# One sequence's recurrent branch recorded behind its attention instead of beside the other's, in batches of two units, and the channel mixer's buffers laid out anew

## What is computed

```
u = rms_norm(h, norm_mix);  proj = u @ w_in        # 1792 wide: q 512 | k 128 | v 128 | xl 512 | gl 512
q, k = rope(rms_norm(q)), rope(rms_norm(k))        # 8 query heads, 2 kv heads, head_dim 64
attn = softmax(q k^T / 8) v                        # no mask, 2048 keys
xc = conv4(xl)                                     # depthwise, centred
for direction in (forward, backward):              # the recurrent branch (RG-LRU)
    r, i = sigmoid(xc @ w_r + b_r), sigmoid(xc @ w_i + b_i)      # block diagonal
    a = exp(-8 r softplus(-lam));  y = scan(a, sqrt(1 - a^2) * (i * xc))
lru = (y_fwd + y_bwd) * gelu(gl)
h = h + concat(rms_norm(attn), rms_norm(lru)) @ w_out
u = rms_norm(h, norm_ffn);  h = h + (silu(u @ w_gate) * (u @ w_up)) @ w_down     # 2816 wide
```

## Time and profile before

| | us |
|---|---|
| median of 3 runs | 2006.09 (2005.65 to 2009.26) |
| the profiled execution | 2005.26 |
| its span, slowest core (core 0) | 2003.7 |
| spans of the eight cores | 1988.4 to 2003.7 |
| TensorE busy | 1791.1 (89%) |
| ScalarE busy | 1074.5 (54%) |
| VectorE busy | 1013.3 (51%) |
| POOL busy | 359.2 (18%) |

### The profile page before, as it was taken

The page is one execution under the profiler, slowest core; times in us unless marked ns, Lnnn a source line. Parts: engine busy times, 40 slices in busy tenths (PEclk is TensorE's granted clock), DMA queues, the critical chain, the costliest instruction groups (busy, mean ns, idle before and its releaser), DMA issues.

```text
span 2003.7 us, 24506 instructions; the slowest of 8 cores (1988.4 to 2003.7 us)
## 1 busy us (share of the span) xinstructions
PE 1791.1 (89%) x8168; PEld 716.1 (36%) x8168; DVE 1013.3 (51%) x1249; ACT 1074.5 (54%) x1350; POOL 359.2 (18%) x396
## 2 busy tenths in 40 slices
PE   6996656866669999999899999999999999999997
PEld 2442212311113333333333334444444444444443
DVE  3477999947884142221522352383473653535331
ACT  4668787799988788766766773121121221113010
POOL 2123654455451221121000000000000000000000
PEclk9998777978789999999999999999999999999999
DMA  8754432572227677685533355476585675664633
GB/s 180 210 155 138 141 99 90 163 188 88 77 69 205 142 155 158 146 206 147 164 89 89 88 159 180 149 225 199 146 267 168 197 230 149 204 196 145 200 108 100
DMA packets 149127, 310.98 MB, mean 155 GB/s; under 512 B 19696, under 2 KB 28016, under 8 KB 149008
## 3 DMA queue, kind: packets, MB, share of 16 engines
q1 hardware_dynamic: 119696, 228.56, 39.1%
q0 software_dynamic: 29312, 80.86, 15.7%
HBM read 263.05 MB, written 69.99 MB: 166 GB/s over the span
## 4 chain that ended last, share of the span: by engine, by line
PE 69%; DVE 10%; ACT 7%; DMA 5%; issue 4%; POOL 4%; SPq 0%; ACTq 0%; POOLq 0%; DVEq 0%
PE ps_all L483 53%; PE ps_all L770 10%; PE ps_all L731 6%; ACT arena L738 2%; DVE arena L807 2%; DMA arena<-xl_d 1%; POOL arena L827 1%; POOL arena L852 1%; DVE arena L843 1%; DMA arena<-xT 1%; DMA xl_d<-arena 1%; ACT arena L820 1%; DMA arena<-rs_d 1%; DVE arena L838 1%; DVE arena L829 1%
## 5 line engine op out<-in xcount | busy, mean ns | idle before, releaser
L483 PE MATMUL ps_all<-arena 128*128 128x512 bf16 (+1 forms) x6120 | 1460.3, 380 | 145.6 <-ACT arena L820 24.9
L483 PEld LDWEIGHTS ps_all<-arena 128*128 128x128 bf16 x6120 | 597.3, 100 | 862.5 <-issue 260.2
L738 ACT ACTIVATE arena<-ps_all 128x1024 bf16<-128x1024 f32 x512 | 507.1, 1029 | 155.6 <-PE ps_all L731 123.6
L770 PE MATMUL ps_all<-arena 128*65 128x512 bf16 x1024 | 393.8, 402 | 18.5 <-DVE arena L746 15.9
L1006 ACT ACTIVATE arena<-ps_all 128x512 f32<-128x512 f32 x176 | 105.1, 597 | 486.2 <-PE ps_all L483 485.7
L1008 DVE SCALAR_TENSOR_TENSOR arena<-arena,ps_all 128x512 f32<-128x512 f32 x176 | 120.7, 686 | 372.5 <-ACT arena L1006 371.0
L1036 POOL DMA_DIRECT2D outT<-arena x64 | 34.6, 540 | 1060.4 <-DVE arena L1034 1050.8
L731 PE MATMUL ps_all<-arena 64*128 64x512 bf16 x1024 | 185.1, 398 | 38.4 <-ACT arena L738 35.0
L1011 DVE SCALAR_TENSOR_TENSOR arena<-arena,ps_all 128x512 bf16<-128x512 f32 x176 | 120.9, 687 | 142.9 <-PE ps_all L483 139.9
L770 PEld LDWEIGHTS ps_all<-arena 128*65 128x65 bf16 x1024 | 108.5, 112 | 210.7 <-issue 151.2
L1034 DVE TENSOR_TENSOR arena<-ps_all,arena 128x512 f32<-128x512 f32 x64 | 43.7, 687 | 159.1 <-PE ps_all L483 159.0
(11 more groups left out here) (59 smaller groups left out, 964.0 us busy)
## 6 DMA issues: line engine op xcount, KB each, us to landing
arena<-wg_s SPq DMA_DIRECT2D x154, 256.0 KB, 2.9
arena<-wu_s SPq DMA_DIRECT2D x154, 256.0 KB, 3.0
arena<-wd_s SPq DMA_DIRECT2D x112, 352.0 KB, 4.6
arena<-xT SPq DMA_DIRECT2D x64, 512.0 KB, 6.5
outT<-arena POOLq DMA_DIRECT2D x64, 256.0 KB, 4.7
arena<-wo_s SPq DMA_DIRECT2D x56, 256.0 KB, 2.7
xl_d<-arena POOLq DMA_DIRECT2D x32, 256.0 KB, 4.0
gl_d<-arena POOLq DMA_DIRECT2D x32, 256.0 KB, 4.6
```

Source lines behind the costliest of these rows:

```text
L483: return P.op("pe", lambda e: e.matmul(t.ap(n) if ap is None else ap(t), lhsT=lhsT, rhs=rhs, start=start, stop=stop), reads=reads, writes= ...
L738: P.op("act", lambda e, i=i, b=b: e.activation(out=Pb[b], in_=T2[i].ap(1024), func=AF.Exp, scale=0.125), reads=[T2[i]], writes=[("Pb", b)] ...
L770: P.op("pe", lambda e, u=u, V=V: e.matmul(O.ap(1024)[0:65, u * 512:(u + 1) * 512], lhsT=V[:, stl, :], rhs=pb[:, u * 512:(u + 1) * 512], st ...
```

## The change

C1 is recorded after B1, and its first convolution operation in each group waits for the last block of sequence 1's attention (`fin[1][15]`). In C1 the four units of a group go in two batches of two, which share two pairs of `ua`/`ut` (C0 still has four). The tiles are laid out anew: the `ua`/`ut` of units 2 and 3, which C1 no longer uses, become `hT[1]` from chunk 1 on; sequence 0's k and V become `mixb[1]`; the attention's own buffers become 4 more `wr` and 3 more `wdb` for chunks 2 and 3; the rest of the recurrent region comes free for chunk 4. So chunks alternate between two `h`/`mix` buffers from the start, and chunk 1 has 6 `wr` and 4 `wdb` (before 12 and 8), chunks 2 and 3 have 10 and 7 (before 12 and 8), and with 2 `tg` (before 4), chunks 4 to 7 have 16 and 11. The bias of -0.5 that put D ahead on the engines other than TensorE is gone.

```diff
         def rec_C(sq, holds):
             P.stream = "C%d" % sq
+            w = {u: u if sq == 0 else UNITS[n % 2] for n, u in enumerate(UNITS)}
...
-                for u in UNITS:
-                    sm, h = u
...
+                for batch in (UNITS,) if sq == 0 else (UNITS[:2], UNITS[2:]):
+                    for u in batch:
...
+                    for u in batch:
+                        P.op("act", lambda e, u=u: e.activation(out=us[u], in_=us[u], func=AF.Sqrt,
...
+                    for u in batch:
...
+                        init = 0.0 if u in UNITS[:2] else (us[prev][:, 0:1] if sm else us[prev][:, 1023:1024])
+                        P.op("dve", lambda e, u=u, rev=rev, init=init: e.tensor_tensor_scan(
+                            out=us[u][:, rev], data0=ua[w[u]][:, rev], data1=ut[w[u]][:, rev], initial=init,
...
-        RL = Region(arena, RCC.start, AD0)
-        hT[1] = RL.alloc([128, 8, 512], F32)
-        mixb[1] = RL.alloc([128, 8, 512], BF16)
+        hT[1] = Region(arena, H1, AD0).alloc([128, 8, 512], F32)
+        mixb[1] = Region(arena, RKV.start, RKV.end).alloc([128, 8, 512], BF16)
+        RL = Region(arena, RCC.start, H1)
+        RBW = Region(arena, RB_.start, RB_.end)
+        wr += [RBW.alloc([128, 8, 128], BF16) for _ in range(4)]
+        wdb += [RBW.alloc([128, NFC // 2, 128], BF16) for _ in range(3)]
...
-        LATE = 1
+        LATE = 4
...
-            hb = 0 if g < LATE else g % 2
+            hb = g % 2
...
-        rec_C(1, ((), (), (), ()))
         rec_B(1, 0)
+        rec_C(1, tuple((fin[1][15],) for _ in range(4)))
         P.handoff(D_EARLY, A_KEYS)
+        P.handoff([("h", 1, k) for k in range(8)], H_KEYS)
+        P.handoff([("mix", 1, k) for k in range(8)], KV_KEYS)
+        P.handoff([("wr", i) for i in range(6, 10)] + [("wdb", i) for i in range(4, 7)],
+                  [(n, b) for n in ("Pb", "qb", "osb", "smb") for b in range(4)])
         P.handoff(D_LATE, C_KEYS)
...
-        for g in range(LATE):
-            stream_d(g)
-            d_load(g)
-            d_out(g)
-            d_gu(g)
-            d_down(g)
-        dc.update(ng=12, nd=8, nt=4)
-        stream_d(LATE)
-        d_load(LATE)
-        d_out(LATE)
-        for g in range(LATE, 8):
+        stream_d(0)
+        d_load(0)
+        d_out(0)
+        for g in range(8):
+            if g == 2:
+                dc.update(ng=10, nd=7)
+            if g == LATE:
+                dc.update(ng=16, nd=11, nt=4)
...
-        out = P.order(pe_rank, dict({"K": -9.0, "A0": -2.0, "C0": -1.0}, **{"D%d" % g: -0.5 for g in range(8)}))
+        out = P.order(pe_rank, {"K": -9.0, "A0": -2.0, "C0": -1.0})
```

More of the change, by code:

```diff
@@ L447, in build @@
         RKV = Region(arena, RC0.ptr, RC0.ptr + 16576)
-        kT = [RKV.alloc([128, S], BF16) for _ in range(2)]
-        V0 = [RKV.alloc([128, 16, 65], BF16) for _ in range(2)]
-        V1 = [RKV.alloc([128, 16, 65], BF16) for _ in range(2)]
+        kT, V0, V1 = [], [], []
+        for _ in range(2):
+            kT.append(RKV.alloc([128, S], BF16))
+            V0.append(RKV.alloc([128, 16, 65], BF16))
+            V1.append(RKV.alloc([128, 16, 65], BF16))
         RB_ = Region(arena, RKV.end, RKV.end + 18688)
@@ L466, in build @@
         lro = RCC.alloc([128, 1024], BF16)
+        ua, ut = {}, {}
+        for n, u in enumerate(UNITS):
+            if n == 2:
+                H1 = RCC.ptr
+            ua[u] = RCC.alloc([128, 1024], F32)
+            ut[u] = RCC.alloc([128, 1024], F32)
         AD0 = RCC.ptr
@@ L812, in rec_C @@
                          reads=[("xc", h)], writes=[("xcb", h)], cost=1.5)
-                for u in UNITS:
-                    sm, h = u
[L815 to L826, removed]
-                    P.op("pool", lambda e, u=u: e.tensor_tensor(out=us[u], in0=ua[u], in1=ua[u], op=ALU.mult),
-                         reads=[("ua", u)], writes=[("us", u)], cost=c_pool(1024))
-                    P.op("dve", lambda e, u=u, h=h: e.scalar_tensor_tensor(
-                        out=ut[u], in0=ut[u], scalar=1.0, in1=xc[h], op0=ALU.add, op1=ALU.mult),
-                        reads=[("ut", u), ("xc", h)], writes=[("ut", u)], cost=1.43)
@@ L888, in build @@
                    + [(n, b) for n in ("ar", "rr0", "rr1") for b in range(2)])
-        D_LATE = ([("mix", 1, k) for k in range(8)] + [("h", 1, k) for k in range(8)]
-                  + [("wr", i) for i in range(6, 12)]
-                  + [("wdb", i) for i in range(4, 8)] + [("tg", i) for i in range(2, 4)])
+        H_KEYS = [(n, u) for n in ("ua", "ut") for u in UNITS[2:]]
+        KV_KEYS = [(n, 0, t) for n in ("k", "V0", "V1") for t in range(4)]
+        D_LATE = ([("wr", i) for i in range(10, 16)]
+                  + [("wdb", i) for i in range(7, 11)] + [("tg", i) for i in range(2, 4)])
         C_KEYS = (["xlp", "halo", "zg", "lro"] + [(n, i) for n in ("xc", "xcb") for i in range(2)]
```

44 lines of the change are left out of this document (27 added, 17 removed).

## The result

The changed kernel takes 1974.0 us (median of 5), the kernel before beside it 2006.1; the ratio is 0.9834 (95% interval 0.9818 to 0.9850), some 33 us. The prediction was 1944, in a range of 1914 to 1980: faster, but by half of what was forecast. The profiled execution took 1972.5 us, its slowest core (core 4) 1970.9.

What follows compares the result with a forecast made beforehand. ScalarE was taken to bound the first six attention blocks, TensorE's work the rest. Terms -10, -103.5, +5, -16.4, +30.2 (matmuls behind the attention) and +33 sum to -61.7 us: 1944 us, own range 1925 to 1962, outer range 1914 to 1980.

Steps and rivals of the forecast that it cites:

- the first six blocks: Attention blocks 1 to 6: exps alone without C1, 15.8 us a block, 95 us instead of 198.5, so -103.5 us.
- chunk 0's start: Chunk 0's sums must go out, be inverted and return while the blocks run faster; +5 us, between 0 and 15.
- the rival of the low clock: First six blocks: TensorE at its lower clock takes 24.5 us a block, 147 us for six; 1996 us, chance 0.05.
- Blocks 7 to 32: Later attention blocks: TensorE at its limit with 76 fewer mixer matmuls by the attention's end; -16.4 us.
- The attention's start: Ahead of the first attention exp: C1's first operations on VectorE and ScalarE go away; -10 us, at most 14.
- the signs that were named: Included 32nd copy near 1103 us, then some 250 us with VectorE above 90% busy, and no more waits behind it.
- VectorE while C1 runs: Behind the attention: overload 11, slower operations 20, chain waits 12, less 10 for PSUM banks; +33 us, ends 0 and 68.
- the 90 us of the strict reading: Rival: each of 39 mixer operations waits out a POOL operation, 90 us instead of 20; 2014 us, chance 0.03.
- The later buffers: Mixer chunks: 4 wr and 3 wdb coming later from the attention, and two tg until chunk 4, cost nothing.
- C1 fully hidden: Rival behind the attention: holes and banks take all of VectorE's excess, +33 becomes 0; 1911 us, chance 0.14.
- The rival that named the batches of two: C1's chain overlaps half as much, VectorE's waits double to 94 us; 2026 us, decides from 95 us on, chance 0.05.
- The holes that stay open in part: Rival behind the attention: all 46.9 us of C1's waits fall on the full VectorE; 1979 us, chance 0.12.

Runs made afterwards that it cites:

- e6: The kernel before with only C1 moved behind B1, one h/mix buffer and the smaller weight buffers until chunk 4; 2087.0 us, ratio 1.0406 to the kernel before.
- e1: The changed kernel without the recurrent branch of sequence 1 (C1), its eight result tiles a constant; 1918.9 us, ratio 0.9548 to the kernel before.
- e9: The changed kernel without the 16 scans of C1; 1966.7 us, ratio 0.9793 to the kernel before.
- e8: The changed kernel with C1's 16 squares on ScalarE instead of POOL; 1968.7 us, ratio 0.9804 to the kernel before.
- e7: The changed kernel with the mixer's bias of -0.5 on the engines other than TensorE given back; 1975.7 us, ratio 0.9845 to the kernel before.
- e4: The changed kernel with 6 wr and 4 wdb for chunks 2 and 3 instead of 10 and 7; 1984.5 us, from one execution.
- e2: The changed kernel with C1's four units in one batch, each with own tiles, and 6 and 4 weight buffers in chunks 2 and 3; 1990.5 us, ratio 0.9914.
- e3: The changed kernel with own tiles for each C1 unit, still batches of two, and 6 and 4 weight buffers in chunks 2 and 3; 1991.5 us, ratio 0.9918.

## Why the prediction was right, and where its size was off

The mechanism was right, and its gain came nearly to the us. ScalarE was the bound of the first six blocks through C1. With C1 gone the exps ran alone: 104.2 us with chunk 0's start, 100 predicted. That the move alone does this is shown by e6, which has it without the rest of the change. The 4 us too many are the blocks': they took (496.90 - 411.93) / 5 = 17.0 us each, not 15.8, with 11.6 us of TensorE's waits for exps in 394 to 497 us and ScalarE busy 91%, while chunk 0's start, +5, cost TensorE 1.0 us of waits. TensorE's clock was 0.98 there, so the rival of the low clock did not come. Blocks 7 to 32 (-16.4) are right within 2.5 us. The attention's start (-10) is right within 0.3 us only between the two slowest cores, 0 and 4, which is luck in part: the same core's first exp came 3.2 to 13.2 us earlier than before, in the median 10.7.

The forecast's own range, 1925 to 1962, missed the 1974; the outer one held it, by the room that was left for the rivals. Of the signs that were named, the 32nd copy came at 1110 us, not 1103, and behind the stretch 4.4 us of waits for L970 stayed.

The step that was off is **"VectorE while C1 runs"**, +33, measured as 38 to 40 (e1). Its size is within the ends 0 and 68, but that it came so near is luck, since the way to it was wrong in four parts. First, VectorE was taken to be over full: 228.8 us of work in 217.8. C1's operations took 129.4 us instead of 139, and the stretch became longer, so VectorE was busy 79%, not over 90%; and the excess wasn't what TensorE paid for, since 39.5 us less of work gave 7 to 8 (e9). Second, the 20 us of slower operations were 8; e8, which takes the squares off POOL, brought them to 3 and gained 4 to 6 in time. By the Trainium skill ("SBUF — State Buffer", Who interferes with whom) a VectorE instruction with two SBUF inputs and a GpSimd instruction that reads SBUF exclude each other. That one scaling fell from 1016 to 744 ns in e8 agrees with it in kind, though another rose from 747 to 1004 beside what POOL still does; the 90 us of the strict reading are nowhere in the trace. Third, VectorE's waits in C1's chain were 28.4 us, not 12. Fourth, TensorE's clock fell to 0.94 in the stretch, in which it stood in waits of 0.2 to 4.4 us, 16.8 us, for which there was no term. The 10 us taken off for the PSUM banks no run tested.

And one term was missing: **"The later buffers ... I cost at nothing"**. Even without C1 the tail was 13 to 15 us longer than before for the same matmuls, most of it in four waits for a chunk's norm around chunks 3 and 4 (11.8 us, against 3.2 before). The bias (e7) is not their cause. The chunks' new buffers, their fewer weights until chunk 4, and the order that follows from both are left as candidates. That the number of weight buffers matters is shown by e4: 12 us for 6 and 4 instead of 10 and 7 in chunks 2 and 3.

Of the rivals, C1 fully hidden did not come, nor a price that decides. The rival that named the batches of two is refuted by e2 and e3, which are no faster with own tiles. The holes that stay open in part are nearest in kind: the 28.4 us lie between the 12 taken and the 47 of that rival.

What the 38 to 40 us of stalls consist of is settled only in part. Leaving out the scans gives 7 to 8 back, the gates 6 to 10, moving the squares 4 to 6, and that these add up was not run; larger batches, own tiles, another order and a third `tg` give nothing. No single wait holds them: take one away, and part of its time comes back at another place of the same order (e2). It fits one schedule written for assumed durations and run in order on four engines, but that was not tested by itself.
